# Window scores as 64x64 products, row sums by additions and three moved steps in a hybrid encoder layer

## What is computed

```
# neighbourhood attention: query row i sees 8 key rows, and of each the columns within a mask
s = einsum('biqhd,birkhd->bhiqrk', q, kg) * (64 ** -0.5)
s = where(col_mask, s + bias, NEG_INF);  prob = softmax(s, axis=(-2, -1))
o = einsum('bhiqrk,birkhd->biqhd', prob, vg)
# latent attention, per head: q, k of 96 channels, v of 64
s = q @ k.T * 96 ** -0.5;  prob = softmax(s);  o = prob @ v
```

## Time and profile before

| | us |
|---|---|
| median of 3 runs | 1569.28 (1569.22 to 1569.84) |
| profiled execution, whole | 1570.64 |
| profiled execution, span | 1568.8 |
| PE busy | 1520.7 (97%) |
| DVE busy | 1043.6 (67%) |
| ACT busy | 636.4 (41%) |
| POOL busy | 345.8 (22%) |
| mean granted TensorE clock | 0.999 |

### The profile page before, as it was taken

One profiled execution on the slowest core, in us unless ns is written; L12 is line 12 of the kernel. 1 busy time (PEld: TensorE's weight loads), 2 busy tenths in 40 slices (PEclk: granted clock), 3 DMA queues, 4 the chain that ended last, 5 costly groups with the idle time before them and its releaser, 6 DMA issues.

```text
span 1568.8 us, 25838 instructions
## 1 busy us (share of the span) xinstructions
PE 1520.7 (97%) x10160; PEld 1101.0 (70%) x10160; DVE 1043.6 (67%) x1503; ACT 636.4 (41%) x1178; POOL 345.8 (22%) x356
## 2 busy tenths in 40 slices
PE   6999999999999999999999999999999999999998
PEld 5788775645555556777754467888888888888786
DVE  7424589778666576666557489775555555689877
ACT  6212246656444444444430225433333333334553
POOL 0900014123410038888810140220000000000000
PEclk9999999999999999999999999999999999999999
DMA  6131010010000010001041012332221211756322
GB/s 245 54 147 53 20 54 14 7 28 13 12 24 12 7 32 3 2 2 29 2 182 74 0 54 69 127 122 86 81 81 54 57 62 44 275 195 207 115 68 108
DMA packets 29001, 110.70 MB, mean 71 GB/s; under 512 B 3568, under 2 KB 6096, under 8 KB 26720
## 3 DMA queue, kind: packets, MB, share of 16 engines
q1 hardware_dynamic: 28432, 103.97, 19.4%
q0 software_dynamic: 464, 5.28, 0.8%
HBM read 89.36 MB, written 18.92 MB: 69 GB/s over the span
## 4 chain that ended last, share of the span: by engine, by line
PE 71%; issue 12%; DVE 9%; POOL 5%; ACT 2%; DMA 1%; DVEq 0%; SPq 0%; POOLq 0%; ACTq 0%
PE psum L2908 24%; PE psum L2925 12%; PE psum L2832 7%; PE psum L2578 4%; PE psum L2605 3%; PE psum L2496 2%; PE psum L2612 2%; PE psum L2515 1%; PE psum L2466 1%; POOL arena L852 1%; POOL arena L854 1%; PE psum L2806 1%; PE psum L2701 1%; PE psum L2719 1%; PE psum L2715 1%
## 5 line engine op out<-in xcount | busy, mean ns | idle before, releaser
L1987 DVE TENSOR_TENSOR part_lo<-arena,part_hi 128x512 fp32r<-128x512 f32 x154 | 117.8, 768 | 77.3 <-ACT part_hi L1268 77.1
L2908 PE MATMUL psum<-h_hi,part_hi 128*128 128x512 f32 x616 | 165.7, 391 | 1.1 <-ACT arena L1316 0.7
L2908 PE MATMUL psum<-h_lo,part_hi 128*128 128x512 f32 x616 | 164.7, 389 | 0.0
L2908 PE MATMUL psum<-h_hi,part_lo 128*128 128x512 f32 x616 | 164.6, 389 | 0.0
L1268 ACT ACTIVATE part_hi<-arena 128x512 fp32r<-128x512 f32 x154 | 95.9, 628 | 132.6 <-PE psum L2908 114.9
L2908 PEld LDWEIGHTS psum<-h_hi,part_hi 128*128 128x128 f32 x616 | 115.2, 188 | 26.7 <-ACT arena L1316 1.1
L2908 PEld LDWEIGHTS psum<-h_lo,part_hi 128*128 128x128 f32 x616 | 115.7, 188 | 24.1
L2908 PEld LDWEIGHTS psum<-h_hi,part_lo 128*128 128x128 f32 x616 | 115.7, 188 | 24.0
L918 POOL TENSOR_TENSOR arena<-arena,consts 128x512 f32<-128x512 f32 x64 | 81.9, 1300 | 135.2 <-ACT arena L1169 134.6
L2832 PE MATMUL psum<-arena 128*128 128x512 f32 x256 | 110.5, 592 | 0.0
L1657 DVE TENSOR_REDUCE stats<-psum 128x1 f32<-128x1024 f32 x64 | 77.8, 1216 | 44.9 <-PE psum L2496 44.7
(11 more groups left out here) (329 smaller groups left out, 3025.7 us busy)
## 6 DMA issues: line engine op xcount, KB each, us to landing
arena<-in_w_gate SPq DMA_DIRECT2D x22, 512.0 KB, 3.7
arena<-in_w_up SPq DMA_DIRECT2D x22, 512.0 KB, 3.7
arena<-in_w_down SPq DMA_DIRECT2D x22, 512.0 KB, 3.6
arena<-in_w_down SPq DMA_DIRECT2D x11, 1024.0 KB, 5.0
arena<-in_w_in SPq DMA_DIRECT2D x15, 512.0 KB, 3.5
arena<-act_spill SPq DMA_DIRECT2D x12, 512.0 KB, 7.0
act_spill<-arena SPq DMA_DIRECT2D x10, 512.0 KB, 6.0
arena<-in_x SPq DMA_DIRECT2D x8, 512.0 KB, 8.1
```

The costliest lines, as they stand in the source:

```text
L1987: v.tensor_tensor(lo, raw[:, at:at + HALF], hi, ALU.subtract).then_inc(part_lo, 1)
L2908: mm = pe.matmul(bank({2: z, 3: y, 5: y}.get(p, x)), w[:, P * k:P * k + P], h[k // 2][:, HALF * (k % 2):HALF * (k % 2) + HALF], start=(fre ...
```

## The change

Three things change.

- **Window scores.** `q_diag` and its copies go. A step with even n computes units n and n+1 in four products of 64 channels, 64 queries and 512 key positions, straight from the projections. Each uses a quarter of the array: rows by e, columns by `rows_of(hp, e)`, which is the same half as e for hp = 0 and the other half for hp = 1. Units rotate over banks 0 to 2; the transposes share bank 3. Bias, transfers of bias and reciprocals, and the reading of the transposes follow the swapped halves (four transfers for the bias where there were two, eight for the reciprocals where there were four).
- **Row sums of heads 4 to 7.** Seven additions per head gather the eight exponential tiles in `e_sums`, on POOL for heads 4 to 6, on DVE for head 7 (six tiles only there). One set of ones products (`sums_of`) follows in the next head behind its first score step. ACT's exponentials wait for the additions that read the ring tile (`summed`).
- **Moved steps.** The reciprocal and transpose of the neighbourhood sums and the memset of `chunk_starts` go behind latent head 1's first guard maximum, and `turned_queries_lo(0, 1)` behind the second. In heads 4 on, `turned_queries_lo` goes to kt = 0. In `scores` the k_hi q_hi product comes last and alone waits for the row maximum. The recurrence operands are interleaved with the reciprocal of head 6 and the additions of head 7. The five memsets go to POOL. Three loops are written out.

```diff
-            for n in range(NU):
-                row, hp = n // 2, n % 2
-                if n >= 2:
-                    pool.wait_ge(na_s_done, n - 1)
-                for e in range(2):
-                    rows = slice(64 * e, 64 * e + 64)
-                    pool.tensor_copy(q_diag[rows, n % 2, 64 * e:64 * e + 64],
-                                     proj[rows, M_NQ + hp, 1 + 64 * row:1 + 64 * row + 64]).then_inc(q_diag_ready, 1)
...
-            pool.wait_ge(prods_ready, PRODS[3])
+            pool.wait_ge(kb_ready, 4)
+            for n in range(HEADS - SUMMED - 1):
+                total = e_sums[n % 2]
+                for kt in range(1, NT):
+                    pool.wait_ge(e_ready, 8 * (SUMMED + n) + kt + 1)
+                    if kt > 1:
+                        pool.wait_ge(summed, 7 * n + kt - 1)
+                    pool.tensor_tensor(total, e_ring[0] if kt == 1 else total, e_ring[kt % NE], ALU.add).then_inc(summed, 1)
+
+            for n, ap in enumerate((*X, *Zs, y_out)):
+                if n == 4:
+                    pool.wait_ge(prods_ready, PRODS[3] - 1)
+                pool.memset(ap, 0.0).then_inc(y_cleared, 1)
...
+                    if add_up and (kt >= NE or first_summed < 2 * i + b):
+                        n = 2 * i + b - first_summed
+                        act.wait_ge(summed, 7 * n + max(kt - NE, 1) if kt >= NE else 7 * (n - 1) + kt + NE)
...
+            def last_head(i):
+
+                v.wait_ge(pr_q, HEADS)
                 v.wait_ge(pr_v, HEADS)
                 v.wait_ge(s_done, 8 * (HEADS - 1))
                 v.wait_ge(kb_ready, 4)
                 v.wait_ge(ex_ready, 16)
...
+                decayed(0)
+                bonus_of(0)
+                decayed(1)
+                invert(i, 0, last=True, add_up=True)
+                add_exps(1)
+                bonus_of(1)
+                add_exps(2)
+                add_exps(3)
+                decayed(2)
+                add_exps(4)
+                add_exps(5)
+                decayed(3)
...
             for n in range(NU + 3):
-                if n < NU:
-                    row, hp, b = n // 2, n % 2, n % 2
+                if n < NU and n % 2 == 0:
+                    row = n // 2
                     first = window(row)[0]
-                    pe.wait_ge(q_diag_ready, 2 * (n + 1))
                     if n >= 2:
                         pe.wait_ge(na_s_biased, n - 1)
-                    pe.matmul(bank(b), q_diag[:, b, :], proj[:, M_NK + hp, 1 + 64 * first:1 + 64 * first + HALF],
-                              start=True, stop=True).then_inc(na_s_done, 1)
+                    for hp in range(2):
+                        for e in range(2):
+                            head_rows = slice(64 * e, 64 * e + 64)
+                            mm = pe.matmul(bank((n + hp) % 3, rows=rows_of(hp, e)), proj[head_rows, M_NQ + hp, 1 + 64 * row:65 + 64 * row],
+                                           proj[head_rows, M_NK + hp, 1 + 64 * first:1 + 64 * first + HALF],
+                                           start=True, stop=True, skip_group_check=True)
+                        mm.then_inc(na_s_done, 1)
...
-                for n, (k_part, q_part, rows) in enumerate(((k_hi, q_hi, 97), (k_hi, q_lo, 96), (k_lo, q_hi, 96))):
+                for n, (k_part, q_part, rows) in enumerate(((k_hi, q_lo, 96), (k_lo, q_hi, 96), (k_hi, q_hi, 97))):
+                    if kt == 0 and n == 2:
+                        pe.wait_ge(max_ready, 2 * i + (b + 1))
...
+            def sums_of(i, b):
+
+                last = 2 * i + b == HEADS - 1
+                pe.wait_ge(summed, 7 * (2 * i + b - SUMMED + 1) - 2 * last)
+                pe.wait_ge(inverted, 2 * i + (b + 2))
+                for g in range(4):
+                    mm = pe.matmul(bank(7, 256, slice(32 * g, 32 * g + 32)), cst(C_ONES)[:, 0:32],
+                                   e_sums[b][:, 256 * g:256 * g + 256], start=True, stop=not last, skip_group_check=True)
```

202 lines of the change are left out of this document (111 added, 91 removed).

## The result

The changed kernel takes **1555.63 us** (median of 4 runs, 1555.16 to 1557.23), the one before beside it 1569.56 (1569.22 to 1571.57): ratio 0.9903, 95% interval [0.9891, 0.9915]. By these medians it is 13.9 us faster, by the ratio 15.2, where the prediction summed up 19.4; the time is inside the predicted range of 1546 to 1557, 5.7 above its point. It is also, almost to the tenth, what the first two rivals forecast (1555.5 and 1555), so the time alone doesn't tell which of the three was right; the trace has to. The profiled execution's span fell from 1568.8 to 1553.7.

The account below looks back on a forecast made before the run. PE was taken to bound the window stage (DVE 9.62 us behind) and later heads. Terms 6.8 + 1.5 + 11.2 - 0.1 = 19.4 off the profiled 1570.64 give 1551.2; the median stands 1.36 lower: 1549.9 us, range 1546 to 1557.

Parts of the forecast that it names:

- the first two rivals: Window scores: only two quarters work at once, 1555.5 us, chance 0.12; row sums: additions cost more, 1555 us, chance 0.13.
- Four quarters at once: Window scores: four quarter-array products overlap, 1.0 us per group; pairs with a guard save 0.64 to 0.83 us each.
- the shared bank 3: Window stage: transposes wait for ACT's copy, but values or scores between them take about as long; no loss counted.
- The bias: Start of window stage: four transfers, whose landing gates the first unit; no cost counted.
- the window term: Window scores: 6.8 us gained, between 4.5 and 8.5.
- The start of head 0: Head 0: five small DVE operations moved behind guard maxima cut PE's 1.82 us wait; 1.5 us gained, between 0.8 and 1.8.
- Row sums: Heads 4 to 7: fifteen ones-product sets at 0.98 removed, four closing groups added; net 11.2 us gained, between 9 and 12.6.
- the second rival: Heads 4 to 7: DVE and POOL additions cost more than they look, some 5 us back, 1555 us; chance 0.13.
- taking turns: Window scores: rival that writers of one bank take turns, group 2.88 us, total 1571.2 us; chance 0.06.
- the end: End of the heads: DVE's and POOL's changed lists stay about level with PE; 0.1 us lost, at most 1.5.

Follow-up runs that it names:

- two transfers: Changed kernel with the neighbourhood bias in two transfers of 128 partitions in place of four of 64: 1552.72 us, ratio 0.9885.
- all that helped: Changed kernel plus bias in two transfers, pair 0's earlier, first window products before first query product, chunk factors after last reciprocal, additions from head 3: 1549.88 us.
- the kernel with the group first: Changed kernel plus bias in two transfers, first window products before head 0's first query product, second query product a unit later, chunk factors after last reciprocal: 1553.63 us.

## Why the prediction was right, and where its sum was off

- **Four quarters at once: right.** 1.02 for the group where 1.0 was taken, starts within 0.02 where 0.2 was said, a pair at 3.94 where 3.9 to 4.1 was said, the stage at 66.27 by the borders of the earlier trace rows where some 66 was said. DVE is busy 94.9% of it where over 95 was said, and 96.7% in the trace with two transfers and a full clock (62.98 of 65.11). Without the two disturbances the stage gains 82.82 less 75.35 = 7.47, inside 4.5 to 8.5. It is made up otherwise than the sum has it: 7.9 came between the first bias addition and the last maximum (73.03 less 65.11), and 0.74 was lost behind it, where the prediction put the shared bank 3 at nothing.
- **The bias: a term put at nothing.** The prediction named the four transfers ("whose landing gates the first unit") and gave them no price. They cost 2.1. The earlier trace rows hid it, since its window begins at 232, behind the end of DVE's wait for the bias at 230.92; that wait, 4.66 in the kernel before, had no row and should have had one.
- **The clock: not in the prediction at all.** All rows of before stood at 1.00, and the sum took every duration at that level. In the changed kernel's trace falls of the clock took 1.66 of the window term (7.47 less 2.13 less 3.68) and 0.87 of the head-0 term. Over all traces it fell in three of the seven with four transfers early in the stage (1.5 to 2.4 us), and at the start of head 0 in ten of the thirteen behind the kernel before (0.7 to 2.1 us against 38.76 where the order of the change stood). What that says of the change is less sure: the fall at head 0 comes without the window scores too, and most executions of the kernel before have a mean granted clock below that of the one trace from which the rows were taken. The trace was a favourable one, and it is only against it that the 2.5 us are lost.
- **The start of head 0: right in its mechanism.** At full clock 40.42 less 38.76 = 1.66 against 1.5; the first guard wait went from 1.82 to nothing, the next is 0.33 (kernel with two transfers), where some 0.5 was said.
- **Row sums: 9.07 against 11.2, one term mis-sized.** The ones products fell from 512 records to 304 as said, and heads 4 and 5 take 30.08 and 30.78 where 29.8 was said. Fifteen sets at 0.98 should have been fifteen at 0.85. The 0.98 was the time from the first ones product to the guard product behind them, and 0.12 of it stays when the set goes: a values step takes 1.86 to the next full-array product where it took 1.74 to the ones products, which use the same column groups as it does. That is 15 x 0.13 = 2.0, nearly the whole difference. The four closing groups cost 0.57, 0.57, 0.57 and 0.45 where 0.52 each was taken (511.11 to 511.68 is one). Of 12.75 less 2.16 = 10.6 came 9.07, so that 1.5 was lost in the heads where 1.4 was set aside (0.9 for late row maxima, 0.5 for DVE and POOL in each other's way): 1.1 of it are PE's waits for maxima (1.9 against 0.8). The additions account for 0.7 in the heads and 1.1 to 1.2 behind them, where nothing was looked for; the second rival, "the additions cost more than they look", was right to fear them, and wrong with its 5 us.
- **The Trainium skill's two rules.** Different row tiles cannot access the same PSUM bank simultaneously (TensorEngine Tiling (Array Packing), Gotcha 1: PSUM Pressure): the trace does not agree for halves that write different partitions of a bank, 1.02 for the group where taking turns would need 2.88. Changing the tiling mode drains TensorE (same page, Key Properties): the 0.12 more that a values step takes on leaving the column groups fits it, though no run shows that the drain is what takes them.
- **The sum again, with what was measured:** window 7.47 less 2.13 less 1.66 = 3.68, head 0 1.66 less 0.87 = 0.79, row sums 9.07, the end less 0.4. That is 13.1, and 1.9 ahead of the changed code, where executions differ by up to 2 us (DVE's latent reciprocal starts at 216.5 to 218.6 in the traces of the same code). Those 1.9 are luck of the two traces; by medians 13.9.

**What stays open:** what lets the clock fall. At head 0 three kernels kept it from 312 to 328 us (two transfers, additions from head 2 on, all that helped), in the one trace each that there is; the kernel with the group first and the one without window scores, with the same wait of 1.56 there, did not. Neither the length of the wait nor PE's busy share ahead of it separates them.

## What to carry to other kernels

When a stage gets shorter, its ends count: put a row in the sum for each wait at the stage's head, here the bias, and for what is left behind its last operation. One trace of the kernel before is one draw of the clock: compare its mean granted clock with those of the other executions before every duration is taken at full level. Cost a removed step by the distance between its neighbours with and without it, not by its own length: 0.85 here and not 0.98. Row sums moved from PE to POOL are good for 2.2 to 3.0 us per head here, less what they cost elsewhere: 6.3 us in heads 0 and 1, clock included, when POOL's other work was crowded there to make room.

## What the hardware showed

- Four 64-row by 64-column products on all quarters of the array, two of them in one PSUM bank on different partitions, run together: eight records of 512 columns in 1.02 us.
- The granted clock fell at head 0 behind waits of PE of 1.5 to 1.8 us in ten of fourteen traces (kernels with and without the window scores), and stayed at 1.00 up to 328 us behind waits of 1.56 to 1.82 in the other four (one of them lost it later, behind 1.87). PE had been busy 80.83 of 82.82 us in the window stage ahead of it in one that kept the clock (the kernel before), 80.83 of 82.86 in one that lost it (without window scores), 69.09 of 75.35 in another that kept it (two transfers) and 69.22 of 77.48 in another that lost it (window scores alone).
- Four transfers of 240 KB to 64 partitions, issued one behind the other in 2.48 us, took 4.4 us to land in the median; the same bytes as two of 480 KB to 128 partitions, issued in 0.80 us, took 3.8.
- DVE and POOL, both with two SBUF inputs: 1.23 became 3.30, 2.45 became 3.30, 0.11 became 1.67; beside POOL's product a scan went from 2.28 to 4.45.
